# Last four tiles in halves with the root applied half by half; weight requests behind the last norm rows and the streams' u behind the last transposes

## What is computed

```
h = rms_norm(x) * norm_g
u, g_pool, v_a, v_b, g_conv = split(h @ w_in, 512 each)
pooled   = trailing means of u over 2/4/8/16 frames, minus u, per group of 128 channels
pool_out = silu(g_pool) * (pooled @ pool_mix) * pool_scale
v        = v_a * sigmoid(v_b)
conv_out = silu(g_conv) * (silu(layer_norm(causal_dwconv31(v))) @ pw_w + pw_b)
y        = x + concat(pool_out, conv_out) @ w_out
out      = rms_norm(y) * final_g      (and the last rows of u and v as states)
```

## Time and profile before

| | |
|---|---|
| Median of 3 runs | 283.54 us (282.57 to 283.54) |
| Profiled execution | 284.08 us |
| Longest span in it (core 3) | 282.7 us; cores 278.7 to 282.7 |
| TensorE busy | 257.5 us, 91% |
| VectorE busy | 180.0 us, 64% |
| ScalarE busy | 151.8 us, 54% |
| GpSimd busy | 60.2 us, 21% |

### The profile page before, as it was taken

How to read it: one execution, slowest core, us unless ns; L and a number is a source line. 1 busy time by engine, 2 the same in 40 slices (tenths; PEclk the granted TensorE clock), 3 DMA queues, 4 the chain that set the end, 5 groups by cost and what they waited for, 6 DMA issues and landing times.

```text
span 282.7 us, 4638 instructions; the slowest of 8 cores (278.7 to 282.7 us)
## 1 busy us (share of the span) xinstructions
PE 257.5 (91%) x1768; PEld 140.0 (50%) x1768; DVE 180.0 (64%) x287; ACT 151.8 (54%) x267; POOL 60.2 (21%) x105
## 2 busy tenths in 40 slices
PE   3376999899899999999999899999999999999980
PEld 1175557657444454444566554545444544454430
DVE  1434244455499999999953595357573874767592
ACT  1343734988832459752299726825716634261453
POOL 0129543534500000007100002102202211121232
PEclk9999989999999899999999999999999999999998
DMA  6999999400799463529399029131435532635324
GB/s 132 310 336 340 327 286 332 129 1 2 85 200 193 148 102 95 92 78 205 70 167 165 5 40 326 27 131 74 150 104 196 212 130 106 215 111 211 151 112 184
DMA packets 22952, 44.37 MB, mean 157 GB/s; under 512 B 9649, under 2 KB 13361, under 8 KB 22802
## 3 DMA queue, kind: packets, MB, share of 16 engines
q1 hardware_dynamic: 21154, 38.90, 45.0%
q0 software_dynamic: 1488, 4.85, 11.0%
q10 hardware_dynamic: 288, 0.33, 0.3%
HBM read 38.00 MB, written 10.93 MB: 173 GB/s over the span
## 4 chain that ended last, share of the span: by engine, by line
PE 64%; ACT 13%; DVE 11%; issue 5%; POOL 3%; DMA 2%; SPq 0%; DVEq 0%; ACTq 0%
PE PS L377 59%; PE PS L381 5%; ACT WT L359 5%; DVE PL L373 3%; ACT HG L428 3%; DMA XA<-xp 2%; DVE HG L373 2%; DVE XR L362 2%; POOL STAT L362 2%; ACT HT L359 2%; DVE PA L362 2%; ACT JUNKB L428 1%; DVE XF L362 1%; ACT LNOT L359 1%; POOL STAT L366 1%
## 5 line engine op out<-in xcount | busy, mean ns | idle before, releaser
L377 PE MATMUL PS<-HT,WIN 128*128 128x512 bf16 (+1 forms) x832 | 149.9, 338 | 4.1 <-ACT HT L359 3.1
L377 PEld LDWEIGHTS PS<-HT,WIN 128*128 128x128 bf16 x832 | 72.3, 101 | 69.5 <-issue 6.5
L366 POOL TENSOR_SCALAR STAT<-STAT 128x1 f32<-128x1 f32 (+2 forms) x34 | 14.1, 414 | 112.9 <-ACT JUNKB L428 71.9
L373 DVE SCALAR_TENSOR_TENSOR HG<-XA,STAT,GB 128x1024 bf16<-128x1024 f32 x16 | 21.9, 1371 | 24.9 <-POOL STAT L362 20.6
L428 ACT ACTIVATE JUNKB<-XR 128x1024 bf16<-128x1024 f32 x13 | 13.8, 1058 | 44.6 <-DVE XR L362 44.6
L359 ACT ACTIVATE WT<-WTAB,PP 128x384 bf16<-128x384 f32 x64 | 33.6, 606 | 0.0
L362 DVE TENSOR_TENSOR XR<-PS,XR 128x512 f32<-128x512 f32 x32 | 22.0, 688 | 17.8 <-PE PS L377 17.8
L377 PE MATMUL PS<-WOUT,PL 128*128 128x512 bf16 x128 | 32.9, 379 | 0.0
L377 PE MATMUL PS<-WOUT,MIXC 128*128 128x512 bf16 x128 | 32.9, 379 | 0.0
L359 ACT ACTIVATE HT<-PS 128x1024 bf16<-128x1024 bf16 x16 | 16.4, 1024 | 17.9 <-PE PS L381 17.7
L377 PEld LDWEIGHTS PS<-WOUT,MIXC 128*128 128x128 bf16 x128 | 12.5, 98 | 15.1
(11 more groups left out here) (107 smaller groups left out, 275.4 us busy)
## 6 DMA issues: line engine op xcount, KB each, us to landing
XA<-xp SPq DMA_DIRECT2D x16, 512.0 KB, 16.0
XR<-xp SPq DMA_DIRECT2D x16, 512.0 KB, 3.6
yp<-XR SPq DMA_DIRECT2D x13, 512.0 KB, 2.8
STG<-w_in SPq DMA_DIRECT2D x12, 512.0 KB, 15.8
vdram<-VST SPq DMA_DIRECT2D x4, 520.0 KB, 5.4
VS<-vdram SPq DMA_DIRECT2D x4, 520.0 KB, 5.8
WIN<-w_in POOLq DMA_DIRECT2D x2, 1024.0 KB, 15.9
WOUT<-w_out POOLq DMA_DIRECT2D x1, 2048.0 KB, 20.2
```

The costliest lines, as they stand in the source:

```text
L366: S.op(eng, lambda e: e.tensor_scalar(out=out, in0=a, scalar1=s1, scalar2=None, op0=op0), reads=reads, writes=writes)
L373: S.op('dve', lambda e: e.scalar_tensor_tensor(out=out, in0=a, scalar=s, in1=b, op0=op0, op1=op1), reads=reads, writes=writes)
L377: S.op('pe', lambda e: e.matmul(out, lhsT=lhsT, rhs=rhs, start=start, stop=stop), reads=reads, writes=writes)
```

## The change

It has two parts. In `last_tiles` the loop takes four tiles (12 to 15) in place of three. `scale` now does one half; the two halves of a tile go into `pend_scale`, and each half of the next tile takes one out, behind its own square. Tile 14 is stored in halves as tile 15 is. The scaling and store of tile 11 (`fin_pend`) stand behind the second square of tile 12. In the front the three loads on GpSimd's queue move behind `pre(15)`, and `u_h` moves behind `trans(15)`, just ahead of `pool_sample`.

```diff
-            for i, p in enumerate(range(NPH - 3, NPH)):
+            for i, p in enumerate(range(NPH - 4, NPH)):
...
                         accum_out=STAT[:, c:c + 1]), reads=[pk, 'STAT'], writes=[ssk, 'JUNKB'])
-                    if i == 0 and hf == 0:
+                    if pend_scale:
+                        pend_scale.pop(0)()
+                    if i == 0 and hf == 1:
                         fin_pend()
                     tt(XF[i][:, sl], xr[:, sl], FGB[:, sl], ALU.mult, [pk, 'FGB'], [fk])
                     if hf == 0:
                         ts(STAT[:, sc:sc + 1], STAT[:, sc:sc + 1], EPS_RMS, ALU.add, [ssk], [ssk], eng='pool')
-                        if pend_scale:
-                            pend_scale.pop()()
...
+                def scale(hf, i=i, p=p, rs=rs, rsk=rsk):
+                    sl = slice(hf * 512, hf * 512 + 512)
+                    fk = 'XF%d_%d' % (i, hf)
+                    if p == NPH - 1 and hf == 1:
+                        ts(XF[i][:, sl], XF[i][:, sl], rs, ALU.mult, [fk, rsk], [fk])
+                    else:
+                        act(XF[i][:, sl], XF[i][:, sl], AF.Copy, [fk, rsk], [fk], scale=rs)
+                    if p >= NPH - 2:
+                        S.op('act' if p == NPH - 1 and hf == 0 else 'sp',
+                             lambda e: e.dma_start(out=yp_d[p][:, sl], in_=XF[i][:, sl]),
+                             reads=[fk], writes=['o_yp%d_%d' % (p, hf)], dma='stl%d%d' % (p % 2, hf))
+                    elif hf == 1:
                         S.op('sp', lambda e: e.dma_start(out=yp_d[p], in_=XF[i][:]), reads=['XF%d_0' % i, 'XF%d_1' % i],
                              writes=['o_yp%d' % p], dma='st%d' % (p % 6))
-                pend_scale.append(scale)
-            pend_scale.pop()()
+                pend_scale += [lambda f=scale: f(0), lambda f=scale: f(1)]
+            while pend_scale:
+                pend_scale.pop(0)()
...
         pre(13)
-        S.op('pool', lambda e: e.dma_start(out=PMW[:], in_=pmw_d), writes=['PMW'], dma='wpm')
-        load_win(12, 16, 'wgp')
-        load_win(16, 20, 'wgc')
-        u_h()
         pre(14)
         v_halo(0)
         v_shuffle(0)
...
         trans(12)
         u_unit(2, 1)
         pre(15)
+        S.op('pool', lambda e: e.dma_start(out=PMW[:], in_=pmw_d), writes=['PMW'], dma='wpm')
+        load_win(12, 16, 'wgp')
+        load_win(16, 20, 'wgc')
         trans(13)
         u_unit(2, 2)
...
         trans(14)
         u_unit(2, 3)
         trans(15)
+        u_h()
         pool_sample()
...
-                if p == NPH - 3:
+                if p == NPH - 4:
                     last_tiles()
```

More of the change, by code:

```diff
@@ L867, in build_program @@
         JUNKB = at(0, "JUNKB", (128, 1024), BF16)[0]
-        XF = [at(16384 + 4096 * i, "XF%d" % i, (128, 1024), F32)[0] for i in range(3)]
+        XF = [at(16384 + 4096 * i, "XF%d" % i, (128, 1024), F32)[0] for i in range(4)]
         S.op('pool', lambda e: e.memset(NEGH[:], -0.5), writes=['NEGH'])
@@ L1115, in build_program @@
         outs = ['o_ys', 'o_st']
-        outs += ['o_yp15_0', 'o_yp15_1'] + ['o_yp%d' % p for p in range(NPH - 1)]
+        outs += ['o_yp%d_%d' % (p, hf) for p in (NPH - 2, NPH - 1) for hf in range(2)] + ['o_yp%d' % p for p in range(NPH - 2)]
         S.op('sp', None, reads=outs)
```

## The result

The whole change takes 281.89 us (median of 6 runs, 281.44 to 282.04), the kernel before 283.49 us (6 runs): a ratio of 0.9945, interval 0.9929 to 0.9962. That is 1.6 us, 0.55%. The forecast was 282.2 us with a range of 281.0 to 283.9; the time lies in it. Of the cases, "faster by over 0.5%" came out, by a hair, where "same" had the larger chance.

What follows compares the result with a forecast made beforehand. TensorE bounds the kernel, held near 139 us by VectorE's stretch from 77 us, then the tail. Tail -1.65 us, front +0.27 (core 3) or +0.76 us (core 1): median 283.54 to 282.2 us, range 281.0 to 283.9.

Steps and rivals of the forecast that it cites:

- faster by over 0.5%: Outcome case for the whole kernel: time falls by more than 0.5% (1.4 us); chance 0.40.
- same: Outcome case for the whole kernel: change within 0.5% (1.4 us), about what a measurement can tell from none; chance 0.55.
- Tail, VectorE: Last tiles: VectorE takes 1.32 us a half against TensorE's 1.72, so the last add starts 0.4 us earlier.
- Tail, ScalarE: Last tiles: with squares and half scalings alternating, the last scaling starts at 277.4 us, not 279.12: -1.75 us.
- the lag: Last tiles: VectorE's last residual add starts 0.4 us behind its matmuls before the change; afterwards this is gone.
- The four tiles: Tail: with tile 12 also in halves, only tile 11's whole-tile scaling remains, and VectorE's lag is gone after two halves.
- Stores: End of kernel: closer half stores add 0.1 us; rival that they land in 3.5 us gives 283.1 us, chance 0.08.
- Requests: Front: moved weight requests start `u_unit(3, 3)` 0.55 us earlier on TensorE; rival that they hold VectorE, chance 0.05.
- Streams' u: Front: its later eviction starts VectorE's `pool_sample` 0.97 us later; at 139 us +0.27 us (core 3), +0.76 us (core 1).
- the debt: VectorE's 0.97 us later start of its long stretch; rival that it is fully absorbed gives 281.9 us, chance 0.20.
- Weights too late: Rival: weights requested 4.9 us later stall `gp_h` near 100 us; slower by over 0.5%, chance 0.05.
- The sum: Core 3: 282.7 - 1.65 + 0.27 = 281.3 us; core 1: 282.3 - 1.65 + 0.76 = 281.4 us; slowest span falls 1.3 us.

Runs made afterwards that it cites:

- e6: Kernel before with one line changed: tile 12's scaling put behind tile 13's second square, still three tiles and whole-tile scalings; ratio 0.9944.
- e8: Kernel before plus the change's tail with three tiles in place of four, front of before; ratio 0.9916.
- e2: Kernel before plus only the change's front (weight requests and streams' u moved), tail of before; ratio 1.0027.
- e3: Kernel before with only the three weight requests moved, streams' u and tail as before; ratio 0.9977.
- e5: Kernel before with only the streams' u (`u_h`) moved behind tile 15's transposes; ratio 1.0020.
- e1: Kernel before plus only the change's tail (four tiles in halves), front of before; ratio 0.9923.
- e4: Whole change with the streams' u (`u_h`) left in its old place; ratio 0.9913 to the kernel before.
- e9: e4 with VectorE's last pooling step of the first pooling loop put one gp unit later; 279.98 us, ratio 0.9880 to the kernel before.
- e12: e9 with the three conv tables requested ahead of the first shuffle; ratio 0.9878 to the kernel before.
- e11: Whole change unaltered, run again on the chip of e9 and e10; 282.04 us, ratio 0.9955 to the kernel before.
- e10: Whole change with VectorE's last pooling step of the first pooling loop put one gp unit later; 279.82 us, ratio 0.9874 to before.

## Why the prediction came out as it did

- **Tail, VectorE.** Right: last add 0.03 us behind the matmuls, tile 11's scaling at 265.27 (worked out: 265.25), tile 13's first add at 267.07 (267.05).
- **Tail, ScalarE.** Right: -1.75 forecast, -1.68 measured. But "On ScalarE the order is the larger part" is only half of it: e6 shows that the one line which lets VectorE catch up gives 1.02 us by itself, since the late root of tile 14 is what the scalings waited for. The 0.4 us that I put down for the lag is the lag at the last add, not what the lag cost.
- **The four tiles.** I gave them the lag's end; e8 shows that three do as well.
- **Stores.** Forecast +0.1 us for the closer queue; from the last scaling to the end it took 3.8 us (median of the cores) against 3.7. The other kernels with this tail have 3.5 to 3.8, so 0.1 us can't be told from none. On cores 4 and 5 of the whole change the span went on for 7.15 and 7.19 us behind the last matmul, 1.2 us more than on the best, in the landing. The closer stores are not the cause: with the tail of before, four cores of e2 have 8.6 to 8.7 us beside 7.8 on the others.
- **Requests.** Right: 0.55 us on TensorE (measured 0.56), and no delay of VectorE beside them.
- **Streams' u.** Right in mechanism and size: the debt 0.97 us forecast, 1.01 measured; the wait at 139 us 1.8 forecast, 1.7 measured; +0.76 us on a core like core 1, 0.66 measured. The +0.27 us for a core like core 3 did not come out, see the sum.
- **Weights too late.** It did not happen for `gp_h`. What I missed stood next to it: I named the conv tables as what the weights meet, and did not ask who reads the tables. Their reader waited 3 to 5 us, by luck under cover. Nor did I see what moving the requests does to the shuffle: "about 1 us earlier" holds for its write, but that write no longer shares its time with the weights, so the read was issued some 10 us earlier (9 to 12 us behind tile 11's transposes, not 21) and met them itself.
- **The sum.** The median fell by 1.6 us (1.3 us on the other chip) where 1.3 was forecast, and that is in part luck: two terms were wrong, and they cancel. The stages give -1.68 + 0.66 = -1.0 us, about -0.9 with the landing. My sum reached -1.3 because it went from core 3, the slowest before, to core 1, and let core 3 absorb 0.7 us of the debt for a rise of 0.27. The whole change has 208.8 us on every core, and in the profile of before cores 2 and 3 had 208.95 and 209.01, at a granted clock of 0.98 from 78 to 123 us. On such a core the front does not add 0.27 us, it takes 0.2 away. No other profiled kernel had such a core (core 1 of e3 was long for another reason), so how often it happens is open.
- **What the sum lacked.** It took the part outside the spans for fixed. Execution time less longest span was 1.3 to 1.5 us in before, e2, e3 and e5, 1.2 to 1.4 with the new tail in three tiles or a part of it (e6 to e8), and 1.0 to 1.1 in every execution of each kernel with four tiles (whole, e1, e4, e9 to e12). With these 0.3 us the sum comes to some -1.2 us. e1 and e8 differ in the code by the fourth tile alone, and have 1.05 and 1.27 us: that much comes with the fourth tile. Why, no row says.

## What to carry to other kernels

When a small piece of work is moved under another engine's wait, follow its eviction, not only its matmuls: here the matmuls were free in both places, and the reader of the eviction was the engine that set the next stage. Where a busy engine's queue releases another, look first at the order in that queue: one long step put behind one short product was worth more (2.0 us of the stretch between e11 and e10) than making everything ahead of it earlier. And after moving a large request, look at every transfer that then shares its time, and at the reader of each.

## What the runs showed of the hardware

GpSimd and VectorE hinder each other in one direction only, in these traces. In the whole change the three requests start at 74.57 us on GpSimd and VectorE's scaling at 74.72; it took 1.28 us, as alone. Nor does a small operation in flight hold VectorE. On core 0, GpSimd's power of one column, then VectorE's gain multiply with two inputs in SBUF, 0.69 us as alone:

```profile
263.61 0.57 POOL L362 TENSOR_TENSOR STAT<-STAT,NEGH 128x1 f32<-128x1 f32 x1
```

```profile
263.73 0.69 DVE L362 TENSOR_TENSOR XF<-XR,FGB 128x512 f32<-128x512 f32 x1
```

The other way round it counts: in e6 the same power, begun while such a gain multiply ran, took 0.94 us in place of 0.57 and ended 0.43 us behind it (275.00 - 274.57).

```profile
273.88 0.69 DVE L362 TENSOR_TENSOR XF<-XR,FGB 128x512 f32<-128x512 f32 x1
```

```profile
274.06 0.94 POOL L362 TENSOR_TENSOR STAT<-STAT,NEGH 128x1 f32<-128x1 f32 x1
```

The Trainium skill (SBUF — State Buffer, "SBUF: two separate sides") has an exclusive lock for the shared port pair, which whichever starts first keeps for its whole instruction; against a VectorE instruction with two SBUF inputs that goes only for a GpSimd operation that reads SBUF. The last pair of rows fits it, the pair at 263 us does not. Whether the request of a load is such an operation is not said there, so the requests are no test of it.

In these traces a transfer that shares its time with the weight loads takes two to four times as long, and which one that is follows from the order of issue. Before, the shuffle's write was issued 3.5 us behind the first request and landed in 13.5 to 14.2 us, and its read, issued when the loads were nearly through, in 5.8 to 7.5 us. In the whole change the write goes out 2.4 us ahead of the requests and lands in 3.0 to 5.8 us; the read, issued 0.8 to 3.6 us behind the first request, in 15.8 to 21.2 us, and on seven of eight cores SP's queue stood still behind it. The Trainium skill (DMA: Bandwidth & Descriptors, "Queues, rings and completion order") has each DMA engine take turns between queues, packet by packet. From 77 to 97 us on core 0 the packets of SP's queue held 380 bytes on average (0.88 MB in 2310) and those of the weights 1880 (2.20 MB in 1173); that the queue with the small packets loses by it fits, though no run here varied the packet size.
